# Making the gated one-hot matrices of a scatter in one VectorE instruction per token

## The reference, cut to what matters

```python
q = (xb @ wq).reshape(C, PEER_HEADS, 2, PEER_DK_HALF)
s = jnp.einsum('chpd,hpnd->chpn', q, keys)
sv, si = lax.top_k(s, K)                                # 16 rows a and 16 columns b per head
cand = sv[:, :, 0, :, None] + sv[:, :, 1, None, :]
cidx = si[:, :, 0, :, None] * N_KEYS + si[:, :, 1, None, :]
top_s, sel = lax.top_k(cand.reshape(C, PEER_HEADS, K * K), K)
eidx = jnp.take_along_axis(cidx.reshape(C, PEER_HEADS, K * K), sel, axis=-1)
g = jax.nn.softmax(top_s, axis=-1)
act = jax.nn.gelu(jnp.einsum('chkd,cd->chk', u_tab[eidx], xb), approximate=False)
return jnp.einsum('chk,chkd->cd', g * act, v_tab[eidx])
```

## Time and profile before

| what | value |
|---|---|
| median of three runs | 2046.31 us |
| the profiled execution, its time | 2046.0 us |
| its span | 2044.2 us |
| TensorE busy | 1985.2 us, 97% |
| VectorE busy | 1490.9 us, 73% |
| ScalarE busy | 979.3 us, 48% |
| GpSimd busy | 1072.0 us, 52% |

### The profile page before, as it was taken

The page is one execution under the profiler, slowest core; times in us unless marked ns, Lnnn a source line. Parts: engine busy times, 40 slices in busy tenths (PEclk is TensorE's granted clock), DMA queues, the critical chain, the costliest instruction groups (busy, mean ns, idle before and its releaser), DMA issues.

```text
span 2044.2 us, 31709 instructions
## 1 busy us (share of the span) xinstructions
PE 1985.2 (97%) x11783; PEld 1771.3 (87%) x11783; DVE 1490.9 (73%) x2883; ACT 979.3 (48%) x1805; POOL 1072.0 (52%) x646
## 2 busy tenths in 40 slices
PE   9999999998999999999999999999999999999998
PEld 8746889998999999999999999999877787877787
DVE  6237538989998388889889999987686635067763
ACT  4337434366788643333333333333556652255643
POOL 3213456865446577776767777674335444411242
PEclk9999999999999999999999999999999999999999
DMA  5330225767679899999999999996322222210021
GB/s 206 81 101 12 74 92 169 260 214 234 236 238 331 316 357 410 399 404 373 365 379 390 412 380 407 365 403 241 117 71 93 83 93 103 94 40 32 21 83 62
DMA packets 155144, 446.78 MB, mean 219 GB/s; under 512 B 14960, under 2 KB 60912, under 8 KB 152816
## 3 DMA queue, kind: packets, MB, share of 16 engines
q1 hardware_dynamic: 108912, 276.96, 38.4%
q0 software_dynamic: 46080, 167.79, 21.2%
HBM read 405.39 MB, written 39.31 MB: 218 GB/s over the span
## 4 chain that ended last, share of the span: by engine, by line
PE 69%; DVE 14%; DMA 6%; issue 5%; POOL 3%; ACT 2%; SPq 0%; DVEq 0%; ACTq 0%
PE bank L528 12%; PE bank L530 12%; PE bank L529 12%; PE bank L934 4%; PE bank L935 4%; PE bank L936 4%; PE bank L915 3%; DMA fetched<-in_u_rows,diag 3%; DVE fetched L2384 2%; POOL wl L2725 2%; DVE wide L2404 2%; PE bank L1156 2%; PE bank L703 1%; POOL fetched L2848 1%; DMA fetched<-in_v_rows,diag 1%
## 5 line engine op out<-in xcount | busy, mean ns | idle before, releaser
L2725 POOL TENSOR_TENSOR wl<-wraw,wh 128x1024 fp32r<-128x1024 f32 x272 | 667.5, 2458 | 660.7 <-ACT wh L1347 658.6
L1347 ACT CAST wh<-wraw 128x1024 fp32r<-128x1024 f32 x360 | 373.3, 1046 | 141.4 <-PE bank L530 109.8
L528 PE MATMUL bank<-WTH,wh 128*128 128x352 f32 x1024 | 336.9, 329 | 22.6 <-issue 22.0
L529 PE MATMUL bank<-WTL,wh 128*128 128x352 f32 x1024 | 334.4, 327 | 0.0
L530 PE MATMUL bank<-WTH,wl 128*128 128x352 f32 x1024 | 334.3, 326 | 0.0
L528 PE MATMUL bank<-AXH,wh 128*128 128x352 f32 (+1 forms) x832 | 299.3, 360 | 5.9 <-issue 4.9
L530 PE MATMUL bank<-AXH,wl 128*128 128x352 f32 (+1 forms) x832 | 294.9, 354 | 0.0
L529 PE MATMUL bank<-AXL,wh 128*128 128x352 f32 (+1 forms) x832 | 294.8, 354 | 0.0
L528 PEld LDWEIGHTS bank<-WTH,wh 128*128 128x128 f32 x1024 | 194.8, 190 | 29.5 <-issue 28.8
L934 PE MATMUL bank<-AXH,wh 128*128 128x352 f32 x576 | 191.8, 333 | 6.6 <-issue 6.6
L529 PEld LDWEIGHTS bank<-WTL,wh 128*128 128x128 f32 x1024 | 194.8, 190 | 0.0
(11 more groups left out here) (557 smaller groups left out, 4109.3 us busy)
## 6 DMA issues: line engine op xcount, KB each, us to landing
wraw<-in_wstream SPq DMA_DIRECT2D x360, 512.0 KB
g_scratch<-gs SPq DMA_DIRECT2D x11, 2048.0 KB, 9.8
gr<-g_scratch SPq DMA_DIRECT2D x15, 1408.0 KB
a_scratch<-tmp SPq DMA_DIRECT2D x72, 176.0 KB
tmp<-a_scratch SPq DMA_DIRECT2D x44, 176.0 KB
sq<-a_scratch SPq DMA_DIRECT2D x28, 176.0 KB
shifted<-hc_scratch SPq DMA_DIRECT2D x12, 270.0 KB, 4.8
h<-in_hT SPq DMA_DIRECT2D x8, 264.0 KB, 5.8
```

The source lines that it names most:

```text
L528: pe.matmul(o, w1, x1, start=n == 0, stop=False)
L529: pe.matmul(o, w1, x2, start=False, stop=False)
L1347: act.copy(wh[n % NSPLIT][:, :], wraw[n % NRAW][:, :]).then_inc(*w_hi.tell(n))
L2725: return pool.tensor_tensor(lo, src, hi.bitcast(F32), ALU.subtract)
```

## The change

ScalarE no longer touches the one-hots. VectorE now makes the plain b matrices of eight tokens (two quads) in one instruction of 1024 elements, still with the numbers 0 to 127 from PSUM, and the gated a matrices with one instruction per token: `tensor_scalar` compares the 128 numbers, now read from SBUF (`iota`, in the tile `cst`), with the token's a, and multiplies by the token's gate. Both are operands with one value per partition, read from `ijgT`. The plain matrices have two buffers of a pair of quads, the gated ones four buffers of a quad. VectorE waits once per pair, for the matmul of the quad before (`scat_mm` of q-3), where it waited for q-4 and for the next in turn. TensorE waits for both `hot` and `hot_gate`.

```diff
-    hots = [sb(B, f"hots{i}", [128, 2, 4, 128]) for i in range(2)]
...
+    hots = [sb(B, f"hots{i}", [128, 8, 128]) for i in range(2)]
+    hots_gated = [below_AXL[:, 0:4, 0:128], below_AXL[:, 4:8, 0:128]]
+    hots_gated += [x[:, 0:512].rearrange("p (i c) -> p i c", i=4) for x in sq]
...
+                pe.wait_ge(*hot.at(q))
                 for i in range(4):
                     pe.wait_ge(*hot_gate.at(4 * q + i))
-                    mm = pe.matmul(bank[:, i * 128:i * 128 + 128], hots[q % 4][1][:, i, :], hots[q % 4][0][:, i, :],
+                    mm = pe.matmul(bank[:, i * 128:i * 128 + 128], hots[q // 2 % 2][:, 4 * (q % 2) + i, :],
+                                   hots_gated[q % 4][:, i, :],
...
-            def gate(q):
-                act.wait_ge(*hot.at(q))
-                for t in range(4 * q, 4 * q + 4):
-                    act.mul(hots[q % 4][0][:, t % 4, :], hots[q % 4][0][:, t % 4, :],
-                            ijgT[:, 2, t:t + 1]).then_inc(*hot_gate.tell(t))
...
-            for q in hots_at(t0):
+            for q in hots_at(t0)[::2]:
...
-                    dve.wait_ge(*scat_mm.at(q - 4))
...
+                    dve.wait_ge(*scat_mm.at(q - 3))
...
-                    dve.tensor_tensor(hots[q % 4][2], iota_psum.unsqueeze(1).unsqueeze(1).to_broadcast([128, 2, 4, 128]),
-                                      places.to_broadcast([128, 2, 4, 128]), ALU.is_equal).then_inc(*hot.tell(q))
...
+                dve.tensor_tensor(hots[q // 2 % 2][:, :, :], iota_psum.unsqueeze(1).to_broadcast([128, 8, 128]),
+                                  ijgT[:, 1, 4 * q:4 * q + 8].unsqueeze(2).to_broadcast([128, 8, 128]),
+                                  ALU.is_equal).then_inc(*hot.tell(q, q + 1))
+                for t in range(4 * q, 4 * q + 8):
+                    dve.tensor_scalar(hots_gated[t // 4 % 4][:, t % 4, :], iota, ijgT[:, 0, t:t + 1], ijgT[:, 2, t:t + 1],
+                                      ALU.is_equal, ALU.mult).then_inc(*hot_gate.tell(t))
```

More of the change, by code:

```diff
@@ L1595, in scatter @@
             blk = t0 // 32
-            def gate(q):
-                act.wait_ge(*hot.at(q))
-                for t in range(4 * q, 4 * q + 4):
-                    act.mul(hots[q % 4][0][:, t % 4, :], hots[q % 4][0][:, t % 4, :],
-                            ijgT[:, 2, t:t + 1]).then_inc(*hot_gate.tell(t))
             now = t0 // 4
-            for q in hots_at(t0):
-                if q < now + 2:
-                    gate(q)
             for q in range(now, now + 2):
@@ L1612, in scatter @@
                          bank_of["scat", q][:, :].rearrange("p (t i) -> p i t", t=4)).then_inc(*scat_out.tell(q))
-            for q in hots_at(t0):
-                if q >= now + 2:
-                    gate(q)
         spilled = [0]
@@ L2326, in scatter @@
                 if q > 3 + EXTRA // 4:
-                    dve.wait_ge(*scat_mm.at(q - 4))
[L2328 to L2340, removed]
-                    dve.tensor_tensor(hots[q % 4][2], iota_psum.unsqueeze(1).unsqueeze(1).to_broadcast([128, 2, 4, 128]),
-                                      places.to_broadcast([128, 2, 4, 128]), ALU.is_equal).then_inc(*hot.tell(q))
+                    dve.wait_ge(*scat_mm.at(q - 3))
+                if q == 34:
+                    dve.wait_ge(*ld_e.at("all"))
+                    dve.scalar_tensor_tensor(eidx2, shared[:, 0:EXTRA], 128.0, shared[:, EXTRA:2 * EXTRA], ALU.mult,
+                                             ALU.add).then_inc(*routed.tell((1, "experts")))
+                    dve.tensor_reduce(token_of, ident.rearrange("p (t a) -> p t a", a=SHARED), AX.X,
+                                      ALU.add).then_inc(*routed.tell((1, "token")))
+                dve.tensor_tensor(hots[q // 2 % 2][:, :, :], iota_psum.unsqueeze(1).to_broadcast([128, 8, 128]),
[4 more added lines that the diff above has]
+                                      ALU.is_equal, ALU.mult).then_inc(*hot_gate.tell(t))
         spilled = [0]
```

## The result

The changed kernel takes 2105.26 us in the median of four runs (2102.72 to 2109.62), against 2046.65 us (also four runs, 2044.93 to 2048.76) before. The ratio is 1.0284, with a 95% interval of 1.0268 to 1.0299: 58.6 us slower.

A forecast was written before the change was run, and what follows sets the result against it. VectorE was taken to bound A and B, with room in C. Dearer pairs plus GpSimd collisions, less credits, gave +15.5, +24 and +12.7, together +52 us on 2046.0, rounded down to 2097 us; range 2061 to 2124 us.

The forecast's parts named there:

- A: Scatter stage from 435 to 512 us, VectorE busy for 74.84 of 77 us; forecast +15.5 us.
- B: Scatter stage from 512 to 604 us, VectorE busy for 88.47 of 92 us; forecast +24 us.
- C: Scatter stage from 604 to 683 us, VectorE busy for 64.79 of 79 us; forecast +12.7 us.
- What a pair costs: A pair of quads takes VectorE 3.17 us, 0.87 more than before: 1.13 plus eight gated one-hots of 0.255 us.
- GpSimd stops it: Gated one-hots reading SBUF wait out GpSimd's subtraction: 2.37 us if it begins among them, 1.18 on average if already running.
- How often: GpSimd's subtractions meet gated stretches at random, costing 9.6 us in A, 14.7 in B and 19.0 in C.
- The two pairs ahead of A: First two of 44 pairs lie before VectorE's 7.3 us wait for the keys' matmul and cost nothing.
- Credits: Picked rows' earlier losses to GpSimd, taken off the sum: 1 us each in A and B, 7 us in C.
- No collision: GpSimd's subtractions fall between the gated stretches, pairs cost only 0.87 us more: +17 us, 2063 us; chance 0.15.
- Every subtraction collides: Each GpSimd subtraction in the scatter stage stops gated one-hots in full: +105 us, 2151 us; chance 0.07 for all or most.
- The faster case: Cheaper VectorE, below 0.146 us per gated one-hot, wins back up to TensorE's 12.2 us idle: 2034 us; chance 0.05.
- Fetches: GpSimd's DMAs need the ports: if some 29 fetches each cost VectorE a third of 0.95 us, about 9 us more.

The follow-up runs named there:

- x5: Changed kernel with the gated one-hots' equality alone, one pointer operand, the multiplication by the gates left out: 2086.89 us.
- x6: Kernel before without ScalarE's 352 multiplications by the gates, TensorE waiting for `hot` instead: 2048.18 us, ratio to before 0.9991.
- x1: Changed kernel with the gated one-hots reading the numbers 0 to 127 from PSUM instead of SBUF: 2074.69 us.
- x2: Changed kernel with GpSimd's subtraction cut to 8 of 1024 columns for the scatter stage's 41 tiles: 2056.99 us.
- x3: Kernel before with GpSimd's subtraction cut to 8 of 1024 columns for 41 weight tiles, as control: 2043.59 us.
- x4: Changed kernel with GpSimd fetching the early picked rows one pick later: 2095.60 us.
- x9: Changed kernel with early fetches two picks later and, on VectorE, the eight gated instructions ahead of the plain one: 2112.25 us.

## Why the prediction was right, step by step

- **VectorE is the bound in A and B, and C has room.** Right. VectorE idled 9.9, 3.5 and 21.0 us in A, B and C before, 0.8, 1.7 and 0 after; time taken off VectorE then came off the kernel (x5: 21 us and 18), and ScalarE's relief was worth nothing that could be measured (x6).
- **What a pair costs.** 0.255 us per gated instruction was worked out and 0.257 measured; the 60 ns of the second pointer were 60 (x5). A pair without collision is 1.13 + 2.06 us against 3.17 predicted.
- **GpSimd stops it.** Shown by x1, where the subtractions stay and only the collisions go, and by x2 against x3: 45 of 58.6 us go with the long subtraction. x1 is needed, since TensorE waits for the subtraction too and a shorter one might help there.
- **How often.** Random arrival was the assumption. Its chance of a collision, n x 2.04 / L + n x 2.37 / L, gives 5.6, 8.5 and 10.9 subtractions that collide in A, B and C, 25 in all. In the trace they were 4, 11 and 14, and 3 more ahead of A: 32, which stopped 28 instructions. The total is near, the pattern is not chance: in C every subtraction collided, so part of the agreement is luck. The price in C was 19.0 us predicted and 32.0 measured. There were 14 subtractions, not 13, all collided, and they begin inside the gated stretch, for 11 of the 13 stopped instructions at the first of the eight, and cost 2.3 us each, not now 2.4 and now 1.2.
- **The two pairs ahead of A.** They were to cost nothing. Three subtractions took 7.1 us from them, and VectorE's wait of 7.3 us for the keys' matmul, which stood behind them, is gone. With their own 0.87 us each that leaves 1.5 us beyond the wait.
- **Credits.** The picked rows were to lose 9 us less in the whole stage; they lost 13.3 before and nothing after, so this term was 4 us short. In A and B it was 1 us each for 3.4 and 2.9.
- **The sum by stretch.** A +15.5 predicted, +13.9 measured; B +24 and +24.1; C +12.7 and +18.8. These are lengths from transposes to transposes. C is the term that was too small, by 6 of the 8 us between 2097 and 2105; the measured stretches add up to 56.8 us. Beside them the profiled execution was 3.1 us late at the start of A and lost 3.7 us after C, in a run that lay 4.4 us over the median. VectorE's own time, after less before in us, counted from one start to the next with the idle time apart:

| stretch | one-hots | of this lost to GpSimd | picked rows | routing and rest | idle | sum |
|---|---|---|---|---|---|---|
| A | +23.9 | 13.3 | -3.4 | +2.5 | -9.1 | +13.9 |
| B | +30.0 | 18.1 | -2.8 | -1.3 | -1.8 | +24.1 |
| C | +48.6 | 32.0 | -8.8 | 0.0 | -21.0 | +18.8 |

The errors of single terms are larger than those of the sums. In B 3.4 us more for collisions met nearly 2 us more from the rows. In C 13.0 us more for collisions met 21.0 us of idle time where 14.1 were counted: 3.1 us for `ijgT`, 3.3 at the stage's end and 0.5 of the wait for the DMA were not in the sum. So the mechanism held, and that the total was only 8 us off is in part luck.

- **The rivals.** "No collision" is x2, 13.4 us over its control where +17 was worked out: near as a price, wrong as a forecast. "Every subtraction collides" came true in C alone, with 32.0 us of collisions there for 30.8. (The lower end of the range was meant to be rival 1's value and stands at 2061 instead of 2063; nothing hangs on it.) The faster case would have needed 0.146 us per gated instruction, where 0.257 was measured.
- **What was to be seen.** 27 gated instructions of over 1 us for "some 20", and ScalarE at half its time, came as said. TensorE stands for 37 us more in this stage (49.6 for 12.2), a little under the 40 to 60.
- **Fetches.** The estimate that followed a rule of the Trainium skill ("SBUF — State Buffer", section "Who interferes with whom"), some 9 us more because GpSimd's own DMAs need the ports, doesn't show beside gated instructions: 15 fetches overlap one in the trace after, and they take 937 to 1015 ns, where most that overlap none take 947 to 954 ns. The test is weak, though: 14 of the 15 overlap only the first of a pair's eight, by about 0.15 us, and the one that ran beside three of them is the one of 1015 ns. Beside a VectorE instruction with two SBUF inputs fetches do get longer. One stands in both kernels (2.76 us in both; here after, VectorE, then GpSimd), and before, two beside picked rows in C took 1.83 and 1.76 us:

```profile
510.20 2.28 DVE L2281 TENSOR_TENSOR spare<-selu,sie 128x2048 uint32<-128x2048 uint32 x1
```

```profile
510.55 2.76 POOL L2832 DMA_INDIRECT fetched<-in_u_rows,diag  x1 [6.34 <-DVE fetched L2368]
```

## What to carry to other kernels

Before moving work onto an engine, look at its busy share in the stage in question, not over the span: VectorE was at 73% over all and at 97% and 96% in A and B, where 25 of the 44 pairs went. An instruction's mean in a quiet stage is not its price beside GpSimd; look in the trace for the same form with GpSimd running, and count the GpSimd instructions that it will meet. Where it must run there, reading from PSUM was better here than reading from SBUF: 0.319 us each, none stopped, instead of 0.257 us and 28 stops of 2.3 us.

## What the runs showed that I had not expected

Cutting GpSimd's instruction into four pieces lowered the loss by only a quarter, since pieces and gated instructions alternate (63 to 48 us lost, and 2105 to 2096 us). Picked rows lost 13.3 us to GpSimd before and nothing after, in x1 0.4, where no gated instruction was ever stopped in their place. That VectorE is the bound is not enough for it: in x4 they lost 4.4 us and in x9, with the gated instructions first, 9.5. The phase of the engines differs between these kernels; what sets it is open. And TensorE's granted clock fell to 0.91 of its upper level (2.4 GHz) over B, from 0.98. From 516 to 522 us, just ahead of B, it was 0.72, after TensorE had stood for 4.2 us; a wait of 6.9 us followed, and within B it waited up to 3.3 us. What this cost is not separated, but VectorE idled for only 1.7 us in B.
